# PEER experts: low parts of the down units on GpSimd, placing rows as per-token operations on VectorE

## The reference, cut to what matters

```python
def chunk(xi):
    q = (xi @ w_query).reshape(B, PEER_CHUNK, PEER_HEADS, 2, PEER_HALF)
    s = jnp.einsum('bthpd,hpnd->bthpn', q, sub_keys)
    s1, i1 = lax.top_k(s[..., 0, :], PEER_TOPK)
    s2, i2 = lax.top_k(s[..., 1, :], PEER_TOPK)
    cand = (s1[..., :, None] + s2[..., None, :]).reshape(B, PEER_CHUNK, PEER_HEADS, PEER_TOPK * PEER_TOPK)
    top_s, top_c = lax.top_k(cand, PEER_TOPK)
    idx = (jnp.take_along_axis(i1, top_c // PEER_TOPK, axis=-1) * PEER_N_KEYS
           + jnp.take_along_axis(i2, top_c % PEER_TOPK, axis=-1))
    g = jax.nn.softmax(top_s.astype(jnp.float32), axis=-1)
    u = jnp.take(expert_down, idx, axis=0)
    act = jax.nn.gelu(jnp.einsum('btd,bthkd->bthk', xi, u).astype(jnp.float32))
    v_sel = jnp.take(expert_up, idx, axis=0)
    return jnp.einsum('bthk,bthkd->btd', (g * act).astype(xi.dtype), v_sel)
```

## Time and profile before

| | |
|---|---|
| median of 3 runs | 3136.68 us (3134.71 to 3142.8) |
| the profiled execution's own time | 3137.76 us |
| its span | 3135.9 us |
| mean granted TensorE clock | 0.98 |
| TensorE busy (matmul) | 3043.5 us, 97% |
| VectorE busy | 2203.9 us, 70% |
| ScalarE busy | 1578.3 us, 50% |
| GpSimd busy | 417.1 us, 13% |

### The profile page before, as it was taken

One profiled execution on the slowest core, in us unless ns is written; L12 is line 12 of the kernel. 1 busy time (PEld: TensorE's weight loads), 2 busy tenths in 40 slices (PEclk: granted clock), 3 DMA queues, 4 the chain that ended last, 5 costly groups with the idle time before them and its releaser, 6 DMA issues. The chain is left out here.

```text
span 3135.9 us, 66433 instructions
## 1 busy us (share of the span) xinstructions
PE 3043.5 (97%) x25756; PEld 2955.6 (94%) x25756; DVE 2203.9 (70%) x3620; ACT 1578.3 (50%) x2760; POOL 417.1 (13%) x319
## 2 busy tenths in 40 slices
PE   9899999999999899999999999999999899999998
PEld 9799988999998799988999999999997799999898
DVE  4669799989996659799978887333255555554654
ACT  5464566655555664566655555232245344444443
POOL 0126322200001016422200000000020000000100
PEclk9999999999999999999999999999999899999899
DMA  6256544578896256644489995323342245555464
GB/s 186 91 162 195 182 144 144 170 261 287 288 363 210 84 160 193 192 142 146 147 270 314 318 313 193 100 94 97 98 113 77 79 137 187 168 192 177 137 193 146
DMA packets 172779, 560.64 MB, mean 179 GB/s; under 512 B 22480, under 2 KB 31440, under 8 KB 172000
## 3 DMA queue, kind: packets, MB, share of 16 engines
q1 hardware_dynamic: 172640, 558.83, 54.8%
HBM read 557.71 MB, written 1.05 MB: 178 GB/s over the span
## 5 line engine op out<-in xcount | busy, mean ns | idle before, releaser
L241 DVE TENSOR_TENSOR peer_e_lo<-raw,peer_e_hi 128x1024 fp32r<-128x1024 f32 x498 | 664.9, 1335 | 127.9 <-ACT peer_e_hi L237 123.7
L237 ACT ACTIVATE peer_e_hi<-raw 128x1024 fp32r<-128x1024 f32 x560 | 588.6, 1051 | 219.6 <-PE peer_e_out L1531 162.3
L241 DVE TENSOR_TENSOR ffn_lo<-raw,ffn_hi 128x1024 fp32r<-128x1024 f32 x256 | 312.9, 1225 | 464.2 <-ACT ffn_hi L237 464.2
L237 ACT ACTIVATE ffn_hi<-raw 128x1024 fp32r<-128x1024 f32 x264 | 279.2, 1061 | 527.0 <-PE ffn_acc L2811 333.1
L1527 PE MATMUL peer_e_out<-x_normed,peer_e_hi 128*128 128x256 f32 x2048 | 493.4, 283 | 3.6 <-ACT peer_e_hi L237 3.4
L1528 PE MATMUL peer_e_out<-x_normed,peer_e_hi 128*128 128x256 f32 x2048 | 481.2, 277 | 0.0
L1594 PE MATMUL peer_e_out<-peer_h_pair,peer_e_hi 128*128 128x256 f32 x2048 | 477.7, 276 | 0.4 <-DVE peer_e_lo L241 0.4
L1595 PE MATMUL peer_e_out<-peer_h_pair,peer_e_hi 128*128 128x256 f32 x2048 | 477.7, 276 | 0.0
L1527 PEld LDWEIGHTS peer_e_out<-x_normed,peer_e_hi 128*128 128x128 f32 x2048 | 385.2, 188 | 8.7 <-issue 8.7
L1528 PEld LDWEIGHTS peer_e_out<-x_normed,peer_e_hi 128*128 128x128 f32 x2048 | 385.4, 188 | 0.0
L1594 PEld LDWEIGHTS peer_e_out<-peer_h_pair,peer_e_hi 128*128 128x128 f32 x2048 | 384.5, 188 | 0.7 <-issue 0.7
(11 more groups left out here) (640 smaller groups left out, 6153.7 us busy)
## 6 DMA issues: line engine op xcount, KB each, us to landing
raw<-in_l_down SPq DMA_DIRECT2D x256, 512.0 KB, 3.6
raw<-in_l_up SPq DMA_DIRECT2D x256, 512.0 KB, 4.8
raw<-in_ffn_wi SPq DMA_DIRECT2D x176, 512.0 KB, 3.7
peer_e_ring<-in_w_mod SPq DMA_DIRECT2D x144, 512.0 KB, 5.2
raw<-in_ffn_wo SPq DMA_DIRECT2D x88, 512.0 KB, 3.6
raw<-in_l_peer_w_query SPq DMA_DIRECT2D x32, 512.0 KB, 3.6
raw<-in_w_in SPq DMA_DIRECT2D x26, 512.0 KB, 3.7
l_in_raw<-in_l_w_in SPq DMA_DIRECT2D x24, 512.0 KB, 4.4
```

Source lines behind the costliest of these rows:

```text
L237: return act.activation(hi, v, ACT.Copy)
L241: return eng.tensor_tensor(lo, v, hi.bitcast(F32), ALU.subtract)
```

## The change

It has three parts, all inside `peer_experts`.

1. From unit 60 on, all low parts of down units are made by GpSimd (`low_down` on GpSimd, 68 per layer) and no longer by VectorE. TensorE and SyncE wait on `lo_pool` instead of `lo_vector` for these.
2. GpSimd's multiplication for plane 2 goes.
3. `make_hots` on VectorE makes all three planes with twelve `tensor_scalar` operations of 128 x 128 per batch: four compare the positions with the second index of a token (plane 1), four with the first index (plane 0), then, after a wait on `plain` (plane 1 done), four multiply plane 1 by the low half of the weight into plane 2. ScalarE waits for `hot`, counted by the last of the twelve.

```diff
@@ wait_lo_down
-            if n >= NS:
+            if n >= ROUTE_AT:
+                eng.wait_ge(lo_pool, NS - BY_VECTOR + n - ROUTE_AT + 1)
+            elif n >= NS:
                 eng.wait_ge(lo_vector, PRE + BY_VECTOR + n - NS + 1)
@@ tensor
+            def score_pool(n, k):
+                score(n, k, lo_pool, n + (NS - BY_VECTOR - ROUTE_AT + 1), used, n - (RAWS - 1 + DIRECT))
...
             for k in range(RING):
-                score_vector(ROUTE_AT + k, k, used, DIRECT)
+                score_pool(ROUTE_AT + k, k)
                 route(k, k, k < G_RING)
             with pe.Fori(1, BATCHES // RING) as i:
                 for k in range(RING):
-                    score_vector(i * RING + (k + ROUTE_AT), k, used, DIRECT)
+                    score_pool(i * RING + (k + ROUTE_AT), k)
                     route(i * RING + k, k)
             for n in range(ROUTE_END, NK):
-                score_vector(n, n % RAWS, used, DIRECT)
+                score_pool(n, n % RAWS)
@@ scalar, weigh_hot
-                act.wait_ge(hot_low, b + 1)
+                act.wait_ge(hot, b + 1)
@@ gpsimd
-            for b in range(BATCHES):
-                pool.wait_ge(hot, b + 1)
-                pool.tensor_tensor(hots[b % RING][:, 2], hots[b % RING][:, 1],
-                                   w_low[:, b * TOKS:(b + 1) * TOKS].unsqueeze(2).to_broadcast([P, TOKS, P]),
-                                   ALU.mult).then_inc(hot_low, 1)
+            for n in range(ROUTE_AT, NK):
+                low_down(n // RAWS, n % RAWS)
@@ vector, make_hots
-                dve.tensor_tensor(hots[b % RING][:, 0:2], iota_half.unsqueeze(1).unsqueeze(1).to_broadcast(both),
-                                  choice[:, 0:2, b * TOKS:(b + 1) * TOKS].unsqueeze(3).to_broadcast(both),
-                                  ALU.is_equal).then_inc(hot, 1)
+                tile, tokens = hots[b % RING], range(b * TOKS, (b + 1) * TOKS)
+                for n in (1, 0):
+                    for a, t in enumerate(tokens):
+                        ins = dve.tensor_scalar(tile[:, n, a], iota_half, choice[:, n, t:t + 1], None, ALU.is_equal)
+                    if n == 1:
+                        ins.then_inc(plain, 1)
+                dve.wait_ge(plain, b + 1)
+                for a, t in enumerate(tokens):
+                    ins = dve.tensor_scalar(tile[:, 2, a], tile[:, 1, a], w_low[:, t:t + 1], None, ALU.mult)
+                ins.then_inc(hot, 1)
@@ vector, the loop over units
             for n in range(NS, NK):
-                if n > NS:
+                if NS < n < ROUTE_AT:
                     low_down(n)
```

More of the change, by code:

```diff
@@ L1269, in peer_experts @@
             st.sem(x) for x in ("v_step", "shifted", "exped", "chosen", "turned", "copied"))
-        hot, hot_low, hot_w, routed, weighted = (
-            st.sem(x) for x in ("hot", "hot_low", "hot_w", "routed", "weighted"))
+        plain, hot, hot_w, routed, weighted = (
+            st.sem(x) for x in ("plain", "hot", "hot_w", "routed", "weighted"))
         hi_up, lo_up, hi_h, lo_h, out_sum = (
@@ L1962, in make_hots @@
             def make_hots(b):
-                both = [P, 2, TOKS, P]
                 if b >= RING:
                     dve.wait_ge(routed, b - RING + 1)
-                dve.tensor_tensor(hots[b % RING][:, 0:2], iota_half.unsqueeze(1).unsqueeze(1).to_broadcast(both),
-                                  choice[:, 0:2, b * TOKS:(b + 1) * TOKS].unsqueeze(3).to_broadcast(both),
-                                  ALU.is_equal).then_inc(hot, 1)
+                tile, tokens = hots[b % RING], range(b * TOKS, (b + 1) * TOKS)
[8 more added lines that the diff above has]
+                ins.then_inc(hot, 1)
             def weigh(b, units):
```

## The result

The changed kernel takes 3328.8 us (median, 3328.36 to 3332.93), the kernel before beside it 3139.7: a ratio of 1.060, with a 95% interval of 1.058 to 1.063. The forecast was 3322 us. The profiled execution's span grew from 3135.9 to 3326.3 us, by 190.4.

What follows compares the result with a forecast made beforehand. VectorE was taken to bound the routing stretches at 3.66 us a unit; 0.94 kept, 1.92 for twelve small operations and 2.27 hold make 5.13, over 126 steps +185 us, giving 3322 us; range 3178 to 3375.

Steps and rivals of the forecast that it cites:

- The place: The two routing stretches, one per layer, 126 steps together, were to carry the whole loss of 185 us.
- The small step: Each of VectorE's twelve tensor_scalar operations per batch was to take 0.160 us, 1.92 us for all twelve.
- The collision: In the routing stretches each GpSimd low part was to stop VectorE's small operations once, for 2.27 us; full exposure had 0.47.
- The copy of 2.20 us: Earlier trace row: a 16-element VectorE copy within SBUF, begun inside GpSimd's low part, ended with it; undisturbed about 0.16 us.
- The hold: The time a GpSimd operation keeps VectorE waiting, put at 2.27 us a unit in the routing stretches.
- Where it falls: GpSimd was to start 2.56 us after a batch's twelfth step, among the last two small operations, nothing hidden beside weigh or use.
- What TensorE waits for: In the routing stretches TensorE's waits were to name GpSimd's low part or ScalarE's rows, its busy share about 62%.
- No collision: Rival, chance 0.10: small operations run beside GpSimd's low part without waiting; 3087 us, or 3073 at four elements a cycle.
- A part of the hold hidden: Rival, chance 0.33: GpSimd's hold begins beside weigh and use, hiding 0.94 us; 3233 us, or 3204 if in each unit.
- ten of twelve: Ten of a batch's small operations were to be through by 2.54 us, just before GpSimd starts at 2.56.
- One element a cycle: Rival, chance 0.05: the twelve small operations take 3.12 us without collision, 4.06 us a unit, +50, 3187 us.
- The clock: Rival, chance 0.03: TensorE's clock falls to 1.2 GHz in the routing stretches, 6.3 us a unit, +333, 3470 us.

Runs made afterwards that it cites:

- the fast version: Changed kernel with the placing rows made by two wide operations, each with one input in PSUM, low parts on GpSimd: 3095 us, 0.982 of the kernel before.

## Why the prediction was right

**The place.** The stretch that was forecast carries 188.9 of 190.4 us, and the edges 1.5.

**The small step.** 0.160 us forecast from two pointer rows, 0.1625 measured; records of about 245 ns where 0.25 was built. The Trainium skill's page "VectorE: DVE Perf Modes" gives a formula in its section on the errata, from which an estimate of 94 ns follows. This trace shows 0.07 us more; the pointer's 0.055 from the earlier trace rows would be the larger part of it, but no run has this operation without a pointer.

**The collision.** The copy of 2.20 us was the right row to stop at. The largest records are 2.42 and 2.43 us, where "near 2.4" stood. The hold is gone without GpSimd's work beside (0.27 us at the longest), gone with a PSUM input (0.41 us), and shrinks one for one with GpSimd's operation. The number of the operations, their form, their type and their speed have each been refused as the cause.

**Where it falls.** From the end of the twelfth step (490.64) to GpSimd's start (493.18) it takes 2.54 us; 2.56 was added up from four latencies. But GpSimd meets the ninth and tenth small operation, not the eleventh. The term that was missing: `use` waits for the `weigh` just ahead of it, which the low part used to cover. `weigh` to `use` is 0.78 us, not 0.60. Against this +0.18 stands the hold, 2.16 us of waiting in place of 2.27: 0.04 of the difference is the step under way when GpSimd starts (493.18 to 493.22), the other 0.07 the estimate from the copy. 0.34 + 0.78 + 1.95 + 2.16 = 5.23, forecast 5.13. The mean over the stretch is 5.158, since the six steps before 402.36 take 26.3 us and not 31.4. The forecast is 7 us off. 3 of them are the kernel before, 3139.7 beside the changed one and not 3136.7; the rest is small because a wait left out, a hold taken too long and the quicker first units, which the forecast did not have, nearly cancel. That part is luck.

**What TensorE waits for** was named wrongly: the waits show `weigh` (85.2 us), not GpSimd's low part or ScalarE's rows. `route` needs `weigh` of two batches before to be done, and `weigh` stands behind the twelve. Its busy share was forecast at 62% and is 71%. The 3.15 us that the forecast divided by the period are TensorE's pace, and its recorded busy time is more: in the kernel before, TensorE already had 217.89 us of it in the 230.40 us from 374.00 to 604.40, 217.89 / 63 = 3.46 a unit. Here it is 3.69, and more where the granted clock is lower: 8.49 us from 490.80 to 501.20 us at 0.84, 6.91 from 511.60 to 522.00 at 1.00.

**The rivals.** No collision: refused by every record over 0.3 us. A part of the hold hidden: it happens in the first units of each stretch and not behind them, and the experiment with eight operations shows it with the period that the sums give. Its condition was worked out wrongly: with a step of 0.148 us the twelfth operation has begun 2.56 us after the batch before, and for all twelve to be through the step would have to be (2.56 - 0.94) / 12 = 0.135; with the 0.78 us it is (2.54 - 1.12) / 12 = 0.118, so the steady part was farther from this case than "ten of twelve" suggests. One element a cycle: the step says otherwise. The clock: it did fall in places, and cost nothing (last section).

**The balance of the change.** Without the hold VectorE would need 3.07 us a unit, TensorE 3.25 as in the fast version (3.15 was taken), and the change would have won an estimated (3.66 - 3.25) x 126 = 52 us. The hold turned this into a loss of 189: by this estimate it costs 241 us. The fast version, which has no hold, won 49.

## What to carry to other kernels

Before work is moved to GpSimd, ask of each VectorE operation beside it where its inputs lie, not how many there are. Here a short operation with one input, input and output in SBUF, waited for the end of GpSimd's subtraction and of its memset alike; one with an input in PSUM passed the subtraction by, even where its step was 0.26 us instead of 0.16. Look in the trace for one small VectorE record that is far too long, and see whether its end is GpSimd's end. Then find out where in the loop it falls by adding the latencies round the loop, since the hold costs only what doesn't fall beside other work. And when an operation is moved away, look for the waits that it had covered.

## What the runs showed of the hardware

Beside the expected: a GpSimd memset, which only writes, holds up small `tensor_scalar` operations as well (0.59 us of waiting for one of 0.95). An operation with two pointer scalars and two calculations has a step of 0.32 us where one with one of each has 0.26, both of 128 elements from PSUM; which of the two costs it is not shown.

TensorE's granted clock was not left untouched, to which the forecast had given 0.03. Three windows of the changed kernel, 5.2 us each, columns as in the earlier trace rows:

```profile
488.40:493.60 5.20, 5.20 (x40) 5.07 (x40) 5.10 (x15) 2.50 (x6) 2.36 (x2) 0.79 0.34 101
569.20:574.40 5.20, 3.59 (x32) 3.27 (x32) 5.09 (x15) 2.49 (x6) 2.39 (x1) 1.00 0.35 101
613.20:618.40 5.20, 5.20 (x36) 5.06 (x35) 5.10 (x15) 2.47 (x7) 2.39 (x1) 0.67 0.29 94
```

From 405 us on TensorE's pauses reach 1.91 us, more than the 0.7 to 1.2 that I had worked out. In some places the mean granted clock falls to 0.79 or 0.67, between the levels of 1.2 and 2.4 GHz, in others it stays at 1.00. It cost nothing: the period is 5.23 us at 490 us and 5.24 on the mean from there to 701 us ((701.33 - 491.76) / 40). At the full clock TensorE needs 3.25 us a unit, as in the fast version, which leaves it 2 us; an estimate for 0.67 is 3.25 / 0.67 = 4.9 us, still less than the period. What tells the two kinds of place apart stays open.
